# Second mixer: who multiplies the rotated heads by their norm's scale, GpSimd or ScalarE

## The reference, cut to what matters

```python
def rms_norm_2(x, g):
    x32 = x.astype(jnp.float32)
    y = x32 * lax.rsqrt(jnp.mean(x32 * x32, axis=-1, keepdims=True) + EPS)
    return (y * g.astype(jnp.float32)).astype(x.dtype)

def apply_rope(x, cos, sin):
    x1, x2 = jnp.split(x32, 2, axis=-1)
    out = jnp.concatenate([x1 * cos - x2 * sin, x2 * cos + x1 * sin], axis=-1)

aq = apply_rope(rms_norm_2(aq.reshape(B, S, A_HEADS, HEAD_DIM), a_q_norm), cos, sin)
ak = apply_rope(rms_norm_2(ak.reshape(B, S, A_HEADS, HEAD_DIM), a_k_norm), cos, sin)
bq = apply_rope(rms_norm_2(bq.reshape(B, S, 2 * B_HEADS, HEAD_DIM), b_q_norm), cos, sin)
bk = apply_rope(rms_norm_2(bk.reshape(B, S, 2 * B_HEADS, HEAD_DIM), b_k_norm), cos, sin)
```

## Time and profile before

| | |
|---|---|
| median of 3 runs | 1805.77 us (1805.67 to 1806.02) |
| the profiled execution's own time | 1807.21 us |
| its span in the profile | 1805.5 us |
| mean granted clock of TensorE | 0.998 of full speed |
| busy share of the span | PE 99%, DVE 61%, ACT 51%, POOL 12% |
| second mixer, first layer | about 1040 to 1200 us of the span |
| second mixer, second layer | about 1424 to 1584 us |

### The profile page before, as it was taken

One profiled execution on the slowest core, in us unless ns is written; L12 is line 12 of the kernel. 1 busy time (PEld: TensorE's weight loads), 2 busy tenths in 40 slices (PEclk: granted clock), 3 DMA queues, 4 the chain that ended last, 5 costly groups with the idle time before them and its releaser, 6 DMA issues.

```text
span 1805.5 us, 23597 instructions
## 1 busy us (share of the span) xinstructions
PE 1787.6 (99%) x8716; PEld 1456.3 (81%) x8716; DVE 1109.0 (61%) x1603; ACT 929.3 (51%) x1273; POOL 225.5 (12%) x254
## 2 busy tenths in 40 slices
PE   9999999999999999999999999999999999999999
PEld 7888877788888888877888877788888877788887
DVE  5555676655555545767555479966554599865553
ACT  6444575544444444666444376555444466644441
POOL 0000131000000000320000096200001383100000
PEclk9999999999999999999999999999999999999999
DMA  9556472565546564644555554536555554555552
GB/s 292 186 186 206 142 209 72 181 192 186 197 153 188 186 218 145 194 133 132 178 191 189 190 192 135 171 133 193 184 186 208 167 171 142 185 159 175 186 190 82
DMA packets 221514, 316.21 MB, mean 175 GB/s; under 512 B 14169, under 2 KB 162289, under 8 KB 221169
## 3 DMA queue, kind: packets, MB, share of 16 engines
q1 hardware_dynamic: 221392, 315.02, 53.4%
q10 hardware_dynamic: 32, 0.01, 0.0%
HBM read 313.94 MB, written 1.05 MB: 174 GB/s over the span
## 4 chain that ended last, share of the span: by engine, by line
PE 91%; DVE 4%; ACT 2%; DVEq 1%; issue 1%; DMA 0%; ACTq 0%; POOL 0%; SPq 0%
PE ps L1905 28%; PE ps L1907 27%; PE ps L1906 27%; PE ps L2042 2%; DVE w_lo L1196 1%; PE ps L1915 1%; PE ps L2146 1%; PE ps L2119 1%; ACT w_hi L704 1%; PE ps L2134 1%; PE ps L2077 1%; DVE score L1679 1%; PE ps L2427 1%; DVEq L1682 0%; PE ps L2442 0%
## 5 line engine op out<-in xcount | busy, mean ns | idle before, releaser
L1196 DVE TENSOR_TENSOR w_lo<-raw,w_hi 128x2048 fp32r<-128x2048 f32 (+2 forms) x296 | 672.7, 2297 | 232.8 <-ACT w_hi L704 231.9
L1905 PE MATMUL ps<-w_hi,aT_hi 128*128 128x512 f32 (+2 forms) x1728 | 688.8, 399 | 2.4 <-DVE w_lo L1357 1.3
L1907 PE MATMUL ps<-w_hi,aT_lo 128*128 128x512 f32 (+2 forms) x1728 | 670.0, 388 | 0.0
L1906 PE MATMUL ps<-w_lo,aT_hi 128*128 128x512 f32 (+2 forms) x1728 | 668.0, 387 | 0.0
L704 ACT ACTIVATE w_hi<-raw 128x2048 fp32r<-128x2048 f32 (+2 forms) x296 | 552.7, 1899 | 157.7 <-PE ps L1907 154.1
L1905 PEld LDWEIGHTS ps<-w_hi,aT_hi 128*128 128x128 f32 x1728 | 325.0, 188 | 78.3 <-issue 17.3
L1907 PEld LDWEIGHTS ps<-w_hi,aT_lo 128*128 128x128 f32 x1728 | 324.7, 188 | 68.1
L1906 PEld LDWEIGHTS ps<-w_lo,aT_hi 128*128 128x128 f32 x1728 | 325.5, 188 | 59.4
L754 ACT ACTIVATE att<-ps,rstd 128x256 f32<-128x256 f32 x132 | 55.4, 471 | 373.8 <-PE ps L1907 373.8
L1276 DVE SCALAR_TENSOR_TENSOR att<-ps,rstd,att 128x256 f32<-128x256 f32 x132 | 57.8, 480 | 282.6 <-ACT att L754 282.6
L1905 PE MATMUL ps<-w_hi,gT_hi 128*128 128x512 f32 x528 | 207.1, 392 | 0.0
(11 more groups left out here) (268 smaller groups left out, 1393.3 us busy)
## 6 DMA issues: line engine op xcount, KB each, us to landing
raw<-in_w_in SPq DMA_DIRECT2D x120, 512.0 KB, 4.5
raw<-in_w_ffn_down SPq DMA_DIRECT2D x88, 512.0 KB, 4.5
raw<-in_w_ffn_in SPq DMA_DIRECT2D x88, 512.0 KB, 5.1
raw<-in_w_ffn_gate SPq DMA_DIRECT2D x86, 512.0 KB, 4.1
raw<-in_w_ffn_up SPq DMA_DIRECT2D x86, 512.0 KB, 5.2
raw<-in_w_ffn_out SPq DMA_DIRECT2D x44, 512.0 KB, 4.6
raw<-in_w_out SPq DMA_DIRECT2D x32, 512.0 KB, 4.7
raw<-in_w_ck SPq DMA_DIRECT2D x8, 512.0 KB, 4.0
```

The lines of the kernel that those rows point to most:

```text
L1196: V.tensor_tensor(o, a, h, ALU.subtract).then_inc(units_split, 1)
L1905: M(o, ah, wh, start=start, stop=False)
L1906: M(o, ah, wl, start=False, stop=False)
L1907: return M(o, al, wh, start=False, stop=stop)
```

## The change

GpSimd keeps the multiplication by the scale for the index key only. For q = 1 to 4 it raises a new semaphore, `turned_pos`, after the rotation, and goes on. ScalarE gets a new step `scaled(q)`, at four written places of its list: it waits for the rotation and for the scale, and then copies each head of each half of the tokens in place (128x64), with the head's column of scales as the copy's scale operand: 2 x 8 = 16 instructions. The last raises `heads_scaled`, for which TensorE now waits. VectorE's one wait before it overwrites space used by the rotation now asks for the last rotation only.

```diff
-                    if scale is not None:
+                    if scale is not None and n == 1:
 
                         pool.wait_ge(head_scale, scale[1])
                         for i in range(2):
...
                     if q == 0:
                         nc.gpsimd.tensor_copy(twice2, heads(proj2[:, :, 1792:1856], 2))
                         nc.gpsimd.drain()
-                    pool.sem_inc(rot_ready, 1)
+                        pool.sem_inc(rot_ready, 1)
+                    else:
+                        pool.sem_inc(turned_pos, 1)
...
+                def scaled(q):
+
+                    n, c0, m0, _ = HEAD_NORMS[q]
+                    act.wait_ge(turned_pos, l * 4 + q)
+                    act.wait_ge(head_scale, l * 5 + q + 1)
+                    for i in range(2):
+                        for h in range(8):
+                            a = proj2[:, i, c0 + DH * h:c0 + DH * h + DH]
+                            o = nc.scalar.activation(a, a, ACT.Copy, scale=ms[:, m0 + 8 * i + h:m0 + 8 * i + h + 1])
+                    o.then_inc(heads_scaled, 1)
...
                 index_relu(2)
+                scaled(1)
                 index_relu(3)
...
                 head_squares(3)
                 win_split(5, 1)
+                scaled(2)
                 item(4)
...
                 evac(5)
                 head_squares(4)
+                scaled(3)
                 item(6)
...
                 diff_out(2)
+                scaled(4)
                 item(8)
...
-                dve.wait_ge(rot_ready, l * 5 + (4 * L + 5))
+                dve.wait_ge(turned_pos, l * 4 + 4)
...
                 def rotated(q):
-                    pe.wait_ge(rot_ready, l * 5 + (4 * L + q + 1))
+                    if q == 0:
+                        pe.wait_ge(rot_ready, l + (4 * L + 1))
+                    else:
+                        pe.wait_ge(heads_scaled, l * 4 + q)
```

More of the change, by code:

```diff
@@ L269, in build @@
         rot_ready = sem("rot_ready")
+        turned_pos = sem("turned_pos")
+        heads_scaled = sem("heads_scaled")
         twice_ready = sem("twice_ready")
```

## The result

The changed kernel takes 1828.6 us (median of 4 runs, 1828.06 to 1829.89) against 1805.89 us before; the ratio is 1.0125 (95% interval 1.0113 to 1.0137). It is 22.7 us slower, where 16.8 us were forecast. The span of its profiled execution is 1826.9 us, 21.4 us longer. The profiled execution of the kernel before was 1.3 us above its median, that of the changed kernel was at it, which is why the medians differ by more than the spans.

The account below looks back on a forecast made before the run. TensorE, busy 99% of the span, bounds the kernel. Per layer, new waits 8.8 plus half clock 4.25 less old losses 4.65 give 8.4 us, 16.8 for two: 1805.8 + 16.8 = 1822.6 us, range 1812 to 1830.

Parts of the forecast that it names:

- wait at q = 1: TensorE waits for ScalarE's copies, which stand behind index_relu(2): 2.0 us a layer.
- wait at q = 2: Copies start near 1087, end near 1090.5, before TensorE comes at 1091.5: hidden, and the old 1.01 us wait gone.
- wait at q = 3: TensorE waits for copies standing behind evac(5) and head_squares(4), which need all of tile 5: 4.1 us a layer.
- wait at q = 4: TensorE waits for copies standing behind diff_out(2): 2.7 us a layer.
- slow clock behind the new waits: TensorE at half clock, 1.7 us each behind q = 3 and q = 4, half behind q = 1: 4.25 us a layer.
- old waits and their clock gone: TensorE's waits at q = 2 and pair_turn(0), with the slow clock behind the latter, disappear: 4.65 us a layer.
- The price of a copy: ScalarE's 128x64 copies with scale column: 0.21 us start to start, 0.33 for the last, 3.5 us a group.
- the relief of VectorE: Without GpSimd beside VectorE's instructions ahead of pair_turn(0), probs(0) is over about 2.1 us earlier.
- A: Waits come, clock falls only behind q = 3, copies 0.17 us apart: 4.05 us a layer, 1813.9 us; chance 0.16.
- D: New and old waits cancel within 3 us, group 2.1 to 2.6 us, no clock fall: 1806 to 1809; chance 0.04.
- B: Copies 0.25 us apart, clock falls after all three waits, no VectorE relief: about 23 us, 1828.7 us; chance 0.16.
- C: Faster if a group takes under 2.1 us without clock falls; 1796.5 us if another ScalarE order hides all; chance 0.04.

Follow-up runs that it names:

- the one with the fixed scale: Changed kernel with its sixteen copies a norm at fixed scale 1.0 instead of the column of scales: 1817.04 us, ratio 1.0061.
- The kernel with the split behind: Changed kernel with one weight unit's split moved from ahead of diff_out(0), evac(5), head_squares(4) and scaled(3) to behind them: 1825.69 us, ratio 1.0109.
- The kernel with GpSimd held back: Kernel before, with GpSimd's last two sums and scaling for q = 3 held until VectorE's probs(0) is done: 1803.53 us, ratio 0.9986.
- one copy: Changed kernel with one of the sixteen copies in each norm, the other fifteen heads not scaled: 1808.38 us, ratio 1.0012.
- The order on ScalarE that it named: Changed kernel with scaled(3) moved behind probs_turned(0) and scaled(4) behind probs_turned(2): 1803.50 us, ratio 0.9983.
- q = 1 alone: Against the kernel before, ScalarE scales only the heads of q = 1, GpSimd the others: 1804.62 us, ratio 0.9988.
- q = 4 alone: Against the kernel before, ScalarE scales only the heads of q = 4, GpSimd the others: 1814.29 us, ratio 1.0042.

## Why the prediction was right or wrong

Direction and mechanism held, and the time lies in the range, near its upper end. The forecast by itself gave 1822.6 us, 6 us too little. By its own steps, for both layers of the profiled executions:

| term | forecast us | measured us |
|---|---|---|
| wait at q = 1 | 4.0 | 4.6 |
| wait at q = 2 | 0 | 0 |
| wait at q = 3 | 8.2 | 10.7 |
| wait at q = 4 | 5.4 | 6.0 |
| slow clock behind the new waits | 8.5 | 10.4 |
| old waits and their clock gone | -9.3 | -9.4 |
| sum | 16.8 | 22.3 (span +21.4, medians +22.7) |

**The price of a copy** was the step that failed most widely. I took 0.21 us from start to start, and it was (3.92 - 0.33) / 15 = 0.24. I had taken the time of 64 columns off the row of 0.25 us. That row also reads PSUM and writes another type, which the copies don't; which of the two makes it cheap for its columns, no run here shows. The rule of the Trainium skill ("ScalarE: Activation LUTs", "What ACT_TABLE_LOAD costs") gives 0.24 us with one pointer operand and 0.15 us without, both estimates for 64 columns; the changed kernel and the one with the fixed scale measure 0.24 and 0.15, and agree. By the measured 0.24 the group is 3.9 us and not 3.5, and the three places should cost 0.43 us more each, 2.6 us in both layers. At q = 1 and q = 4 the waits grew by 0.3 us each and not by 0.43, as the copies began some 0.15 us earlier against TensorE than I had placed them.

**The wait at q = 3** had a second part. "At best" ScalarE would have copied the second half of tile 5 at the tile's end. In fact its pair of copies began at 1109.97, the second about 0.6 us later, when tile 5 had been over since 1109.2 (TensorE was at its place for q = 3 at 1110.6, and two steps of 0.68 us lie between). Before, TensorE ran at half clock between `pair_turn(0)` and the end of tile 5, and ScalarE's chain (exponentials, split, `diff_out(0)`) had that time; as the slow clock went, ScalarE became the later one. The kernel with the split behind shows the backlog by itself: 5.5 became 4.4 us in the first layer and 5.2 became 4.4 in the second. So about 1 us a layer of what the clock gave back was not gained.

**The clock.** I counted 1.7 us behind every wait of q = 3 and q = 4 and half of that behind q = 1. Behind q = 1 the clock fell in one layer of two, as forecast. Behind the others it cost 2.6 and 1.7 us in the first layer and 1.4 and 3.0 us in the second: two of the four stretches lasted about 7 us and not 3.4, the first of them with 1.7 us inside the wait itself. Their sum was 8.7 against 6.8 us. Why some last longer stays open. The 3.4 us of slow clock that the forecast took off came from a profiled execution with more of it than most others (0.998, where 0.999 is the commonest); most executions had less of it to lose.

**What went.** The waits at q = 2 and `pair_turn(0)` went in both layers, and the relief of VectorE came as worked out: 1.06 and 1.08 us in the two rows. The kernel with GpSimd held back shows its cause without any work on ScalarE: the same two rows take 0.16 and 0.67 us there.

**The rivals.** A had the clock fall only behind q = 3, with shorter copies: refuted by 0.24 us and by the stretches behind q = 4. D, new and old waits cancelling within 3 us, is refuted by +22.7 us. B forecast 1828.7 us from 0.25 us a copy, a fall of the clock behind all three waits, and no relief of VectorE. Its time was hit, and its first part; its third was wrong, and its second held in one layer only. So B hit the time partly by luck: ScalarE's backlog at q = 3, which neither case had, made up for what it had wrong. C, faster, was refuted for these places; its point of 2.1 us a group was also too kind, as even one copy (0.33 us) at these places makes 1808.4 us. The order on ScalarE that it named does bring the change to 1803.5 us. No run reached its 1796.5 us, all waits hidden: the wait at q = 1 stays in that kernel, and where the waits at q = 1 and 2 went, TensorE waited for VectorE at `pair_qk(0)`.

## What to carry to other kernels

When a step moves to another engine, its price is set first by the place in that engine's list: ask what stands in front of it, and when TensorE wants the result after that. At a place well ahead of the need the sixteen copies cost nothing; at a place just before it they cost their whole length, as the kernels with shorter copies and with one copy show. The same 128 copies made this kernel 1.25% slower or 0.17% faster. A wait of TensorE of some two microseconds can cost twice, once as a wait and once as the clock behind it; in the profiled executions of several versions that win here the waits only moved and the gain is the clock's. The other executions leave more than that to be explained. And a list with two engines near their bound gives little back: what is won at one wait is lost at the next, so look for the second-latest releaser before a gain is counted.

## What was not expected of the hardware

In the stretches read here GpSimd's two-input instructions cost VectorE, and are stretched themselves: a product of one column took 1.22 us beside one and 0.16 us without, and GpSimd's 128x512 took 3.27 us beside a split of VectorE's and 1.28 us where no split stood. Moving these instructions by 3 to 5 us moved the loss to `pair_turn(1)` instead of ending it. The same wait is not always followed by half clock: behind that of 2.3 us at q = 1 it came in one layer and not in the other of the changed kernel, and in both with q = 1 alone; behind that of 2.3 us at `pair_qk(0)` with one copy, in neither; with q = 4 alone, behind that of 1.9 us at `pair_turn(0)` and that of 3.0 us at q = 4, in one layer each. Waits of 0.4 to 1.5 us in the two mixers' profiles were never followed by it. ScalarE's copies of 64 columns from SBUF stand 0.15 us apart with a fixed scale and 0.24 with a column of scales.
